# A hyena core written out as four crossed units, with filter halves as sum and difference, on one core of a Trainium2 chip

## The reference, cut to what matters

```python
def hyena_mixer(h, w_in, conv_w, conv_b, f_w1, f_b1, f_w2, f_b2, f_w3, f_freq, skip, w_out, z, decay):
    Bsz, L, D = h.shape
    u = dwconv3(h @ w_in, conv_w, conv_b)
    v, x1, x2 = jnp.split(u, 3, axis=-1)
    a = jnp.sin(f_freq * (z @ f_w1 + f_b1))
    a = jnp.sin(f_freq * (a @ f_w2 + f_b2))
    filt = (a @ f_w3).astype(jnp.float32).reshape(L, HY_ORDER, 2, D) * decay[:, None, None, :]
    fwd = filt[:, :, 0]
    bwd = filt[:, :, 1]
    k2 = jnp.concatenate([fwd, jnp.zeros_like(fwd[:1]), bwd[1:][::-1]], axis=0)
    k2 = k2 / jnp.sum(jnp.abs(k2), axis=0, keepdims=True)
    kf = jnp.fft.rfft(k2, axis=0)
    gates = (x1, x2)
    zc = v
    for o in range(HY_ORDER):
        zf = jnp.fft.rfft(zc.astype(jnp.float32), n=2 * L, axis=1)
        y = jnp.fft.irfft(zf * kf[None, :, o], n=2 * L, axis=1)[:, :L]
        zc = gates[o] * (y.astype(h.dtype) + skip[o] * zc)
    return zc @ w_out
```

## Time and profile before

| | |
|---|---|
| median of 3 runs | 3224.53 us (3221.63 to 3225.21) |
| profiled execution, its own time | 3216.0 us |
| its span, first to last instruction | 3214.1 us |
| mean granted TensorE clock | 0.951 |
| TensorE busy | 2951.6 us (92%) |
| VectorE, ScalarE, GpSimd busy | 1375.7, 700.9, 1676.0 us |

### The profile page before, as it was taken

How to read it: one execution, slowest core, us unless ns; L and a number is a source line. 1 busy time by engine, 2 the same in 40 slices (tenths; PEclk the granted TensorE clock), 3 DMA queues, 4 the chain that set the end, 5 groups by cost and what they waited for, 6 DMA issues and landing times.

```text
span 3214.1 us, 39121 instructions
## 1 busy us (share of the span) xinstructions
PE 2951.6 (92%) x14667; PEld 2361.3 (73%) x14667; DVE 1375.7 (43%) x1922; ACT 700.9 (22%) x1053; POOL 1676.0 (52%) x1594
## 2 busy tenths in 40 slices
PE   7997899999899999999989989999898776799998
PEld 7885898779877877888865567888685443578886
DVE  5575665221152066333345643330354676343312
ACT  2373222343251001111014631110111111021100
POOL 6651332455307665666652136667574454466663
PEclk9997999999999999999989999999998888899999
DMA  3221000122102345556531012332221100223331
GB/s 117 66 66 34 1 0 0 53 78 70 62 1 79 117 160 184 182 181 193 188 123 40 27 53 79 98 107 90 72 92 56 33 17 0 74 84 92 92 108 62
DMA packets 291653, 259.59 MB, mean 81 GB/s; under 512 B 6329, under 2 KB 263958, under 8 KB 291276
## 3 DMA queue, kind: packets, MB, share of 16 engines
q1 hardware_dynamic: 287840, 248.53, 24.8%
q0 software_dynamic: 2256, 6.55, 0.6%
q10 hardware_dynamic: 1436, 2.96, 0.3%
HBM read 255.92 MB, written 2.10 MB: 80 GB/s over the span
## 4 chain that ended last, share of the span: by engine, by line
PE 77%; DVE 9%; issue 7%; POOL 3%; ACT 2%; DVEq 2%; POOLq 1%; DMA 1%; ACTq 0%; SPq 0%
PE ps L486 20%; PE ps L487 20%; PE ps L488 20%; PE ps L1474 2%; DVE cv L1913 2%; PE ps L1122 1%; PE ps L1135 1%; DVE HN L618 1%; PE ps L1141 1%; PE ps L1352 1%; PE ps L1362 1%; PE ps L1484 1%; PE ps L1342 1%; DVE HNL L611 1%; PE ps L785 1%
## 5 line engine op out<-in xcount | busy, mean ns | idle before, releaser
L486 PE MATMUL ps<-HNH,spl 128*128 128x512 f32 (+1 forms) x2496 | 912.7, 366 | 65.7 <-DVE HNL L611 24.6
L487 PE MATMUL ps<-HNL,spl 128*128 128x512 f32 (+1 forms) x2496 | 898.7, 360 | 0.0
L488 PE MATMUL ps<-HNH,spl 128*128 128x512 f32 (+1 forms) x2496 | 894.4, 358 | 0.0
L685 POOL CAST spl<-raw 128x512 fp32r<-128x512 f32 (+1 forms) x352 | 249.1, 708 | 743.8 <-PE ps L488 566.5
L486 PEld LDWEIGHTS ps<-HNH,spl 128*128 128x128 f32 x2496 | 478.2, 192 | 173.4 <-issue 67.3
L487 PEld LDWEIGHTS ps<-HNL,spl 128*128 128x128 f32 x2496 | 479.0, 192 | 70.5 <-issue 2.9
L687 POOL TENSOR_TENSOR spl<-raw,spl 128x512 fp32r<-128x512 f32 (+1 forms) x352 | 500.9, 1423 | 56.3 <-issue 6.8
L488 PEld LDWEIGHTS ps<-HNH,spl 128*128 128x128 f32 x2496 | 478.3, 192 | 70.1
L691 POOL TENSOR_TENSOR spl<-raw,spl 128x512 fp32r<-128x512 f32 (+1 forms) x352 | 478.3, 1359 | 51.5 <-issue 1.5
L689 POOL CAST spl<-raw 128x512 fp32r<-128x512 f32 (+1 forms) x352 | 229.0, 650 | 221.2 <-PE ps L488 217.6
L486 PE MATMUL ps<-AFH,spl 128*128 128x512 f32 x528 | 207.4, 393 | 0.0
(11 more groups left out here) (415 smaller groups left out, 4237.3 us busy)
## 6 DMA issues: line engine op xcount, KB each, us to landing
adw<-in_ada_w SPq DMA_DIRECT2D x96, 512.0 KB, 5.5
raw<-in_w_in SPq DMA_DIRECT2D x44, 1024.0 KB, 5.2
raw<-in_ffn_w_up SPq DMA_DIRECT2D x88, 512.0 KB, 4.7
raw<-in_w_ffn_in SPq DMA_DIRECT2D x44, 512.0 KB, 5.1
raw<-in_ffn_w_down SPq DMA_DIRECT2D x16, 1408.0 KB, 6.1
raw<-in_hy_w_in SPq DMA_DIRECT2D x12, 1024.0 KB, 5.0
raw<-in_w_ffn_out SPq DMA_DIRECT2D x8, 1408.0 KB, 6.7
raw<-in_w_branch_dn SPq DMA_DIRECT2D x8, 1024.0 KB, 4.9
```

What stands on the lines that cost most here:

```text
L486: pe.matmul(dst, w[0], x[0], start=first, stop=False)
L487: pe.matmul(dst, w[0], x[1], start=False, stop=False)
L488: return pe.matmul(dst, w[1], x[0], start=False, stop=final)
L685: pool.tensor_copy(hi[:, first, :], w[:, first, :])
```

## The change

It has one large part and two small ones.

1. The four units are written out across each other. While unit u is multiplied, TensorE transforms unit u + 1's filter and makes unit u + 2's. On each engine the order of work is a list of calls.
2. `W3` now has forward and backward weights on 128 partitions, and `A1` holds the network's output twice, once with the lower half negated. So TensorE gives the filter's sum and difference at once, and `FB` with two VectorE passes per tile goes. |fwd| + |bwd| becomes max(|sum|, |difference|), on VectorE instead of GpSimd. The filters of unit 0 are made inside `hy_in`, which is written out instead of looped; the second layer of the filter network too.
3. ScalarE writes Z's even part straight into `XZ` (no `ZS`), makes the skip term, and the high part `ZH` for the output projection. The last inverse is done by frequency half, in eight half banks.
4. Tables go into the raw slots as `hy_in` leaves them; `hy_out`'s first slab is loaded after the last Z, the second after the last inverse.
5. Small: norms over 512 tokens write compact tiles `HSH`, `HSL`, `HS` (row length 512) in place of `HNH`, `HNL`, `HN` (528); two rows of constants are loaded twice.

The diff, cut to its core (lines on the SBUF layout, semaphores and small helpers are left out):

```diff
+        HSH = at("HSH", [KD, SEQ], hn_at, dtype=F32R)
+        HSL = at("HSL", [KD, SEQ], lo_at, dtype=F32R)
+        HS = at("HS", [KD, SEQ], lo_at)
...
-                    sp.wait_ge(acc_ready, hy_out.u0)
-                    for buf, src in ((t_fwd, A["t_fwd"]), (t_inv, A["t_inv"])):
-                        sp.dma_start(buf[:, :, :, :].rearrange("p s k n -> p (s k n)"), src).then_inc(table_full, 16)
-                    sp.wait_ge(y_inv, 1 + 2 * ORDERS * NT)
+                    sp.wait_ge(split_ready, hy_in.last(10))
+                    sp.dma_start(t_fwd[:, :, :, :].rearrange("p s k n -> p (s k n)"), A["t_fwd"]).then_inc(table_full, 16)
+                    sp.wait_ge(split_ready, hy_in.last(11))
+                    sp.dma_start(t_inv[:, :, :, :].rearrange("p s k n -> p (s k n)"), A["t_inv"]).then_inc(table_full, 16)
+                    sp.wait_ge(y_dft, 2 * UNITS)
                 done += [gm.last(r) for r in range(gm.nslab)]
                 turns, rest = gm.nslab // R, gm.nslab % R
                 for r in range(min(R, gm.nslab)):
                     if gm.s0 + r >= 2:
                         sp.wait_ge(split_ready, done[gm.s0 + r - 2])
+                    if gm is hy_out and r == 1:
+                        sp.wait_ge(y_inv, UNITS * NT)
...
+            filter_in(0)
+            pool_split(pool, hy_in)
+            pool.wait_ge(y_pm, NT)
+            filter_in(1)
+            k_parts(0, 0)
+            k_parts(0, 1)
+            y_parts(0, 0)
+            pool.wait_ge(y_pm, 2 * NT)
+            filter_in(2)
+            for u in range(UNITS):
+                if u:
+                    y_parts(u, 0)
+                if u + 1 < UNITS:
+                    k_parts(u + 1, 0)
+                y_parts(u, 1)
+                if u + 1 < UNITS:
+                    k_parts(u + 1, 1)
+                if u + 3 < UNITS:
+                    pool.wait_ge(y_pm, (u + 3) * NT)
+                    filter_in(u + 3)
...
+            def k_transform(u, f):
+                if f:
+                    pe.wait_ge(y_kc, 2 * u + 1)
+                else:
+                    pe.wait_ge(y_pm, (u + 1) * NT)
+                    if u >= 2:
+                        pe.wait_ge(y_rn, u + 1)
+                        pe.wait_ge(y_z, (u - 1) * NT)
...
+            pe.wait_ge(y_pm, NT)
+            turn_in(0)
+            pe.wait_ge(table_full, 32)
+            pe.wait_ge(y_rn, 1)
             taken(pe, hy_in, 2, 2 * R - 1)
             taken(pe, hy_in, 2, 2 * R - 2)
+            k_transform(0, 0)
+            z_transform(0, 0)
+            k_transform(0, 1)
+            pe.wait_ge(y_kc, 2)
+            filter_tile(1, 0, 0)
+            filter_tile(1, 1, 2)
+            z_transform(0, 1)
+            pe.wait_ge(y_pm, NT + 1)
+            filter_tile(1, 2, 0)
+            pe.wait_ge(y_pm, NT + 2)
+            filter_tile(1, 3, 2)
+            for u in range(UNITS - 1):
+                if u:
+                    z_transform(u, 0, u + 1)
+                k_transform(u + 1, 0)
+                if u:
+                    z_transform(u, 1)
+                k_transform(u + 1, 1)
+                if u == 0:
+                    pe.wait_ge(y_x, 2)
+                    filter_norm(1, 6)
+                turn_in(u + 1)
+                if u + 2 < UNITS:
+                    filters(u + 2)
+                else:
+                    z_transform(u + 1, 0)
+                inverse(u)
+            u = UNITS - 1
+            z_transform(u, 1)
+            pe.wait_ge(y_x, 2 * UNITS)
+            pe.wait_ge(y_z, u * NT)
+            for f in range(2):
+                pe.wait_ge(y_y, 2 * u + f + 1)
                 for c in range(NT):
+                    for e in range(2):
+                        mm = y_products(ps[:, (4 + c, LAST_ODD[c])[e], 0:SEQ // 2], c, e, f)
+                    if f:
                         mm.then_inc(y_inv, 1)
+            pe.wait_ge(y_z, u * NT + 1)
...
+            turned_in(0)
+            k_out(0, 0)
+            z_even(0, 0)
+            k_out(0, 1)
+            filter_abs(1, 0)
+            filter_abs(1, 1)
+            z_even(0, 1)
+            filter_abs(1, 2)
+            for u in range(UNITS):
+                if 0 < u < UNITS - 1:
+                    z_even(u, 0)
+                if u + 1 < UNITS:
+                    k_out(u + 1, 0)
+                if u:
+                    z_even(u, 1)
+                else:
+                    filter_abs(1, 3)
+                if u + 1 < UNITS:
+                    k_out(u + 1, 1)
+                    turned_in(u + 1)
+                if u + 2 == UNITS:
+                    z_even(u + 1, 0)
+                skipped(u, 0)
+                skipped(u, 1)
+                if u + 2 < UNITS:
+                    filter_abs(u + 2, 0)
+                    skipped(u, 2)
+                    filter_abs(u + 2, 1)
+                    skipped(u, 3)
+                    filter_abs(u + 2, 2)
+                    filter_abs(u + 2, 3)
+                else:
+                    z_hi(u, 0)
+                    skipped(u, 2)
+                    z_hi(u, 1)
+                    skipped(u, 3)
+                    z_hi(u, 2)
+                    z_hi(u, 3)
...
+            def filter_out(u, t, b):
+                if t == 0:
+                    dve.wait_ge(y_w, 48 * (u + 1))
+                    if u:
+                        dve.wait_ge(y_ab, u * NT)
+                dve.wait_ge(y_f, u * (NT + 1) + t + 1)
+                dve.tensor_tensor(PM[:, 0, t, :], ps[:, b, :], DEC[:, t, :], ALU.mult)
+                dve.tensor_tensor(PM[:, 1, t, :], ps[:, b + 1, :], DEC[:, t, :], ALU.mult).then_inc(y_pm, 1)
+            def filter_sum(u, t):
+                dve.wait_ge(y_ab, u * NT + t + 1)
+                x, y = AB[:, 0, :], AB[:, 1, :]
+                if t == 0:
+                    if u:
+                        dve.wait_ge(y_f, u * (NT + 1))
+                    dve.tensor_tensor(AS[:, :], x, y, ALU.max).then_inc(y_n, 1)
+                else:
+                    dve.tensor_tensor(x, x, y, ALU.max)
+                    dve.drain()
+                    dve.tensor_tensor(AS[:, :], AS[:, :], x, ALU.add).then_inc(y_n, 1)
+                dve.drain()
...
+            def multiply(u, f):
+                dve.wait_ge(y_zc, 2 * u + f + 1)
+                dve.drain()
+                dve.tensor_tensor(XZ[:, 2, :], XZ[:, 0, :], ps[:, 5, :], ALU.subtract)
+                dve.tensor_tensor(XZ[:, 3, :], ps[:, 7, :], XZ[:, 1, :], ALU.subtract)
+                dve.drain()
+                dve.tensor_tensor(XZ[:, 0, :], XZ[:, 0, :], ps[:, 5, :], ALU.add)
+                dve.tensor_tensor(XZ[:, 1, :], XZ[:, 1, :], ps[:, 7, :], ALU.add).then_inc(y_x, 1)
+                dve.drain()
+                dve.wait_ge(y_kp, 2 * u + f + 1)
+                if u or f:
+                    dve.wait_ge(y_y, 2 * u + f)
...
+            multiply(0, 0)
+            filter_out(1, 0, 0)
+            filter_out(1, 1, 2)
+            filter_sum(1, 0)
+            filter_sum(1, 1)
+            filter_out(1, 2, 0)
+            filter_out(1, 3, 2)
+            multiply(0, 1)
+            filter_sum(1, 2)
+            filter_sum(1, 3)
+            norm_out(1, 6)
+            for t, b in enumerate((0, 2, 6, 4)):
+                filter_out(2, t, b)
+            gated(0, lambda c, y: whole(c % 2, y))
+            norm_out(2, 2)
+            multiply(1, 0)
+            multiply(1, 1)
+            for t, b in enumerate((0, 2, 6, 4)):
+                filter_out(3, t, b)
+            gated(1, lambda c, y: whole(c % 2, y))
+            norm_out(3, 2)
+            multiply(2, 0)
+            multiply(2, 1)
+            multiply(3, 0)
+            gated(2, whole)
+            multiply(3, 1)
+            gated(3, by_parity)
```

518 lines of the change are left out of this document (254 added, 264 removed).

## The result

| | before | after |
|---|---|---|
| median of the runs | 3224.53 us (3221.63 to 3225.21) | 3128.31 us (3128.08 to 3132.91) |
| span of the profiled execution | 3214.1 us | 3125.9 us |
| mean granted clock | 0.951 | 0.963 |
| last product of the input projection to first of the output projection | 325.5 us | 231.5 us |

The ratio is 0.9707 (95%: 0.969 to 0.9723): 96.2 us less by the medians and 94.5 by the ratio, where 76.7 were forecast.

The account below looks back on a forecast made before the run. Handovers in one row, not an engine, bind the hyena core: 7.9 + 88.4 + 56.3 + 89.5 + 8 = 250.1 us against 326.8. The 76.7 less, off the 3224.5 median, gives 3148, own range 3132 to 3164, with two rivals 3114 to 3178.

Parts of the forecast that it names:

- compact HS tiles: 0, at most 2 either way: Norm output tiles made compact: same count and size, so worth 0, at most 2 us either way.
- Input projection +7.9: Unit 0's filters and norm move into the hyena layer's input projection and add 7.9 us there, nothing else.
- The rival in which the filters stall TensorE by 22 us: Input projection: four filter tiles wait for VectorE and ScalarE, 22 us, kernel 3170; chance 0.05.
- a core of 250 us: Sign: 250 us from the input projection's last product to the output projection's first, at mean clock above 0.9.
- Into unit 1: Core from the input projection's end to the end of unit 0's inverse: 88.4 us, with TensorE waits of 4 and 5.9.
- Unit 1: Core's second piece, to the end of unit 1's inverse: 56.3 us, TensorE and the chain VectorE-GpSimd about level.
- Tail: Unit 2 and the rest, up to the output projection: 89.5 us, with TensorE waits of 6.7 and 5.7.
- The clock's 8 us: Core: slow TensorE work after waits, four places that matter at 2 to 3 us each, counted as 8 us.
- Collisions: Core: VectorE beside GpSimd on SBUF tiles, 1.05 us charged to VectorE per pair; such operations near 1.1 us in the mean.
- TensorE as the bound: Rival for the core: only TensorE's work and the tail's fixed waits are left, 222 us, kernel 3120; chance 0.17.
- VectorE and GpSimd as the bound: Rival for the core: all GpSimd operations collide, eight products some 3.2 us longer each, 25 us, kernel 3173; chance 0.17.
- The low clock: Rival: the core stays at 1.2 GHz, 102 us more, kernel 3327, slower than before; chance 0.03.

Follow-up runs that it names:

- strided: Changed kernel with the norm's output tiles HSH, HSL, HS back in rows of 528 words, as before the change: ratio to before 0.9769.
- before_compact: Kernel before with the compact tiles alone, its hyena core untouched: 3205.19 us, ratio to before 0.9952.
- align_work: Changed kernel with the feed-forward input tiles AFH and AFL placed 16 words (64 B) lower: 3127.7 us, ratio to before 0.9712.
- shift64: Changed kernel with the compact tiles HSH, HSL, HS placed 16 words (64 B) further on: 3136.6 us, ratio to before 0.9737.
- best_a: Changed kernel with VectorE making all core sums, SyncE fetching unit 0's last filter layer, and three edits of VectorE's order: 3117.38 us, ratio to before 0.9681.
- dve_sums: Changed kernel with GpSimd's 16 sums per unit (KP, YF) given to VectorE, behind the product they belong to: ratio to before 0.9694.
- late_slab: Changed kernel with the first slab of the output projection's weights fetched only when the last inverse is done: ratio to before 0.9743.

## Why the prediction was right, and where its size was off

**The mechanism** was right: the core was bound by handovers in a row, and written out across units it is bound by TensorE with a few fixed waits. Of the 206.4 us of TensorE's work in the forecast, 7.9 moved into the input projection, so 198.5 are the core's own. Measured are 209.0 busy us, of which 8.6 are the low clock (below), so 200.4. What is shown by runs is the worth of the tiles, of the early slab and of the sums on GpSimd. That the rest comes from the crossed order is read from the traces, in which the waits of the earlier trace rows are gone; no run has the crossed order without the filters as sum and difference, or these without it, so how the 74 to 79 us divide between the two is open.

**The size was met in part by luck.** The measured 3128.3 us lie 4 us below the forecast's own range of 3132 to 3164; they are inside only the wider range that takes in the rivals. And without the compact tiles the change is worth 74 us (strided) to 79 (against before_compact), with the forecast's 76.7 between them, but as a sum of two errors that nearly cancel: the core came out 10.7 us shorter than its 242.2, and the input projection some 8 us longer than put, as shown below.

**The term that was mis-sized** is "compact HS tiles: 0, at most 2 either way". They are worth 15.4 us alone and 20 when taken away, and 3456 of their 4032 matmuls lie in stretches that I said would not move (the other 576 are the input projection's). By the forecast's own sign it would be wrong "if other stretches of the kernel move by more than a few us", and they moved by 6.6 and 7.0: this part of it was wrong. I had bounded the tiles by count and size, and the trace of before held nothing on layout; the bounds should have been open.

**Input projection +7.9.** The sign to look for was "longer by 8 us", and it is longer by 13.2. Against before_compact, whose stage took 148.1 us, the changed kernel's 164.2 is 16 more. Of it 3.6 are the DMA issues (put at 0 to 2, with the prediction trusting the cover of VectorE's norm). The rest is the forecast's 7.9, 0.9 for the second layer of the filter's network, which the new order moved in too and I left in the core, and waits of 1.01 and 1.58 us for VectorE that I took as none. These make 15.0 of the 16.1 us; what is left is about what the products behind the second wait lost at the low clock.
```profile
2386.79 1.99 PE L1439 MATMUL ps<-W,A 128*128 128x512 f32 x4 [1.01 <-DVE A L2492]
...
2444.60 1.23 PE L1446 MATMUL ps<-ones,AS 128*128 128x1 f32 x8 [1.58 <-DVE AS L2513]
```
The rival in which the filters stall TensorE by 22 us is out.

**Core, forecast 242.2 with its clock, measured 231.5.** The forecast's list of signs names "a core of 250 us" from projection to projection; that is a slip, since 7.9 of the 250.1 stand inside the input projection. The core took 231.5 in this execution and 236 to 239 where the long branch of the first unit was met (align_work, strided, shift64). Into unit 1: 88.4 against 84.0; the 5.9 us before the norm are 0 in one branch and 4.47 in the other, the 4 us before K are 2.42. Unit 1: 56.3 against 56.1, with the wait in the transposes 3.29 (4.3 forecast) and none before the inverse. Tail: 89.5 against 91.4, with waits of 5.87 and 2.86 (6.7 and 5.7 forecast) and 5.7 of the clock's 8.6 us. With the clock's share taken off each piece, the forecast was too dear by 6.2, 1.3 and 3.8 us. The clock's 8 us were 8.6: 1.8, 1.1, 1.6, 2.65 and 1.45 from the five slow groups above.

**Collisions** were charged too high: VectorE's operations on SBUF tiles have a mean of 0.90 us in the core, not the 1.1 given as a sign. Each collision costs what was said, as in align_work's first unit (VectorE, then GpSimd):
```profile
2508.49 1.75 DVE L2556 TENSOR_TENSOR YB<-YB,YT 128x512 f32<-128x512 f32 x1
```
```profile
2507.97 1.71 POOL L950 TENSOR_TENSOR KP<-KS 128x512 f32<-128x512 f32 x1
```
There are fewer of them on SBUF tiles than I let meet. The Trainium skill (SBUF — State Buffer, section "Who interferes with whom") calls the shared ports an exclusive lock for a whole instruction. By that rule dve_sums would take away every such pair with GpSimd's work, and its trace agrees: of its 200 such operations none is above 1.4 us. Any other way of sharing would give the same there, so this does not single out a lock.

**Rivals.** TensorE as the bound (3120) is nearer to the measured time than the forecast's 3148, but only by the tiles. Its 222 us hold the 7.9 that moved, so its core is 214.5, 17 below the measured 231.5; the forecast's is 10.7 above. The truth lay between the two, and best_a with 226.5 is further on that way. VectorE and GpSimd as the bound (3173) is out: no inverse of units 0 to 2 waits for YF. The low clock did not hold: 0.95 over the core.

**Output weights** went as forecast: late_slab gives 11.6 us back. The start DMAs and the straight-line code, put at 0, can't be seen apart from the rest; no run isolates them.

## What to carry over

When one chain of short handovers binds, write the next unit's independent work into it and count again from TensorE's own work: here that number, 198.5 us for what stayed in the core, was good to 1%. Give an edit of layout an open range, or measure it alone, even if no instruction changes. And where two engines share SBUF, moving small sums onto the other engine's queue need not cost time: here it was 4 us less, within the noise, with 5.5 us in the trace's core. Look up first what the longer queue delays.
